# Layer norm of a two-layer trunk: variance summed with tokens on partitions, root and reciprocal once for each token

## What is computed

```python
def layer_norm(x, g, b):
    xc = x - jnp.mean(x, -1, keepdims=True)
    var = jnp.mean(xc * xc, -1, keepdims=True)
    return xc * lax.rsqrt(var + LN_EPS) * g + b

# layer l, m = SiLU(cond) @ w_mod[l] + b_mod[l]
x <- layer_norm(ALPHA * x + 0.5 * gate0 * swiglu(modulate(x, m, 0)))
x <- layer_norm(ALPHA * x + gate1 * mixer(modulate(x, m, 1)))        # conv, then DeltaNet
x <- layer_norm(ALPHA * x + 0.5 * gate2 * swiglu(modulate(x, m, 2)))
# conv mixer: ... a = silu(layer_norm(dwconv(a))) ; a @ w2 + b2
```

## Time and profile before

| | before |
|---|---|
| median of 3 runs | 1921.97 us |
| lowest, highest | 1919.72, 1922.42 us |
| profiled execution, its time | 1926.03 us |
| profiled execution, its span | 1924.3 us |
| PE busy | 1811.4 us, 94% |
| DVE busy | 1028.3 us, 53% |
| ACT busy | 788.7 us, 41% |
| POOL busy | 265.9 us, 14% |
| DMA, mean over the span | 132 GB/s |

### The profile page before, as it was taken

The page is one execution under the profiler, slowest core; times in us unless marked ns, Lnnn a source line. Parts: engine busy times, 40 slices in busy tenths (PEclk is TensorE's granted clock), DMA queues, the critical chain, the costliest instruction groups (busy, mean ns, idle before and its releaser), DMA issues.

```text
span 1924.3 us, 30512 instructions
## 1 busy us (share of the span) xinstructions
PE 1811.4 (94%) x11079; PEld 1664.8 (87%) x11079; DVE 1028.3 (53%) x1780; ACT 788.7 (41%) x1238; POOL 265.9 (14%) x317
## 2 busy tenths in 40 slices
PE   5999999987799999999999999899899999999998
PEld 3899999676578999988999998888788867999997
DVE  4433444899683344455444448766555447443444
ACT  2333332655453444235444326454444335444322
POOL 2000000576320000010000003000222222000001
PEclk8999999998899999999999999999899889999999
DMA  9764444754556443456444445422000024444440
GB/s 323 220 217 129 118 135 142 252 191 126 170 197 207 127 127 114 140 168 195 131 129 117 135 142 146 131 56 66 9 11 11 11 92 130 118 122 131 133 127 35
DMA packets 369962, 254.13 MB, mean 132 GB/s; under 512 B 9716, under 2 KB 350308, under 8 KB 369892
## 3 DMA queue, kind: packets, MB, share of 16 engines
q1 hardware_dynamic: 369104, 252.89, 43.2%
q10 hardware_dynamic: 787, 0.32, 0.1%
HBM read 250.55 MB, written 2.62 MB: 132 GB/s over the span
## 4 chain that ended last, share of the span: by engine, by line
PE 76%; DVE 14%; issue 3%; ACT 2%; DMA 2%; SPq 1%; DVEq 0%; POOL 0%; ACTq 0%
PE bank L1476 22%; PE bank L1478 22%; PE bank L1477 22%; DVE conv L1065 3%; PE bank L1539 2%; DVE tap_odd L1065 2%; DVE w_lo L969 2%; DMA mod_raw<-in_w_mod 1%; SPq L458 1%; PE bank L1747 1%; DVE rstd L1033 1%; PE bank L1503 1%; PE bank L1681 1%; PE bank L1715 1%; PE bank L1724 1%
## 5 line engine op out<-in xcount | busy, mean ns | idle before, releaser
L1476 PE MATMUL bank<-h_hi,w_hi 128*128 128x384 f32 x1920 | 656.2, 342 | 5.6 <-POOL h_lo L587 3.0
L1478 PE MATMUL bank<-h_hi,w_lo 128*128 128x384 f32 x1920 | 645.4, 336 | 0.0
L1477 PE MATMUL bank<-h_lo,w_hi 128*128 128x384 f32 x1920 | 645.0, 336 | 0.0
L969 DVE TENSOR_TENSOR w_lo<-w_raw,w_hi 128x1024 fp32r<-128x1024 f32 x336 | 430.5, 1303 | 191.3 <-ACT w_hi L712 189.6
L712 ACT ACTIVATE w_hi<-w_raw 128x1024 fp32r<-128x1024 f32 x336 | 344.3, 1050 | 314.4 <-PE bank L1478 295.0
L1476 PEld LDWEIGHTS bank<-h_hi,w_hi 128*128 128x128 f32 x1920 | 362.9, 189 | 40.3 <-issue 31.1
L1477 PEld LDWEIGHTS bank<-h_lo,w_hi 128*128 128x128 f32 x1920 | 363.1, 189 | 0.1
L1478 PEld LDWEIGHTS bank<-h_hi,w_lo 128*128 128x128 f32 x1920 | 362.6, 189 | 0.0
L1478 PE MATMUL bank<-act_hi,w_lo 128*128 128x384 f32 x704 | 235.9, 335 | 0.0
L1477 PE MATMUL bank<-act_lo,w_hi 128*128 128x384 f32 x704 | 235.8, 335 | 0.0
L1476 PE MATMUL bank<-act_hi,w_hi 128*128 128x384 f32 x704 | 235.8, 335 | 0.0
(11 more groups left out here) (305 smaller groups left out, 1796.2 us busy)
## 6 DMA issues: line engine op xcount, KB each, us to landing
w_raw<-in_ffn_w_in SPq DMA_DIRECT2D x176, 512.0 KB, 4.7
mod_raw<-in_w_mod SPq DMA_DIRECT2D x132, 512.0 KB, 5.5
w_raw<-in_ffn_w_out SPq DMA_DIRECT2D x64, 448.0 KB, 3.5
w_raw<-in_ffn_w_out SPq DMA_DIRECT2D x32, 512.0 KB, 3.7
w_raw<-in_dn_w_in SPq DMA_DIRECT2D x32, 512.0 KB, 4.0
w_raw<-in_cv_w SPq DMA_DIRECT2D x24, 512.0 KB, 4.1
mod_early<-in_w_mod SPq DMA_DIRECT2D x12, 512.0 KB, 9.7
w_raw<-in_dn_w_out SPq DMA_DIRECT2D x8, 512.0 KB, 4.0
```

The costliest lines, as they stand in the source:

```text
L969: dve.tensor_tensor(w_lo[:, slot], w_raw[:, slot], w_hi[:, slot].bitcast(F32), ALU.subtract).then_inc(w_lo_ready, 1)
L1476: pe.matmul(ps, w_hi[:, w_slot, k], a_hi, start=start, stop=False)
L1477: pe.matmul(ps, w_hi[:, w_slot, k], a_lo, start=False, stop=False)
L1478: return pe.matmul(ps, w_lo[:, w_slot, k], a_hi, start=False, stop=stop)
```

## The change

The variance is summed with the tokens on the partitions. Each of the three blocks of 128 tokens is the stationary operand, a column of `mean_w` the moving one: six products of one column give three columns of variances, one token to a partition, in the free columns T to T+NT of the same bank. ACT and DVE take root and reciprocal of these 128 x 3 values into a new tile `tok_rstd`. PE then spreads them: for each block, `tok_rstd`'s column repeated over 128 columns is the stationary operand and the identity the moving one, which puts the value of token t into column t on all partitions. The result stays in PSUM (`rstd_ps`, columns 0 to T of bank 5), and the multiplies of `normalise` and of the conv module read it there.

A semaphore `tok_ready` tells PE that the reciprocal is there; `rstd_ready` is now given by PE. On PE only slice 4 of the first group stays right behind the variance products; slices 5 to 7 come behind the spread. Where there is no group, 3 warming products take the place of 2 and 10. At the end 6 warming products take the place of 10, and no longer behind a wait.

```diff
+        tok_rstd = sb("tok_rstd", [P, NT])
...
-        mean_ps, var_ps = bank[4], bank[5]
+        mean_ps, var_ps, rstd_ps = bank[4], bank[5], bank[5][:, 0:T]
...
+        tok_ready = sem("tok_ready")
...
                 act.wait_ge(var_added, norm + 1)
-                act.activation(rstd[:, :], var_ps[:, 0:T], ACT.Sqrt, bias=eps[:, :]).then_inc(dev_ready, 1)
+                act.activation(tok_rstd[:, :], var_ps[:, T:T + NT], ACT.Sqrt, bias=eps[:, :]).then_inc(dev_ready, 1)
...
                 dve.wait_ge(dev_ready, norm + 1)
-                dve.reciprocal(rstd[:, :], rstd[:, :]).then_inc(rstd_ready, 1)
+                dve.reciprocal(tok_rstd[:, :], tok_rstd[:, :]).then_inc(tok_ready, 1)
                 dve.wait_ge(rstd_ready, norm + 1)
...
-                    dve.tensor_tensor(conv[:, o], conv[:, o], rstd[:, :], ALU.mult).then_inc(conv_normed, 1)
+                    dve.tensor_tensor(conv[:, o], conv[:, o], rstd_ps, ALU.mult).then_inc(conv_normed, 1)
...
-                    dve.tensor_tensor(r[:, o], r[:, o], rstd[:, :], ALU.mult).then_inc(normed, 1)
+                    dve.tensor_tensor(r[:, o], r[:, o], rstd_ps, ALU.mult).then_inc(normed, 1)
...
-                for j, done in enumerate((sum_g, sum_v)):
+                for done in (sum_g, sum_v):
                     pe.wait_ge(done, 3 * norm + 3)
-                    mm = pe.matmul(var_ps[:, 0:T], mean_w[:, :], squares_at[4 * j], start=(j == 0), stop=(j == 1))
+                for t in range(NT):
+                    for j in range(2):
+                        mm = pe.matmul(var_ps[:, T + t:T + t + 1], squares_at[4 * j][:, t * P:(t + 1) * P], mean_w[:, 0:1], start=(j == 0), stop=(j == 1))
                 mm.then_inc(var_added, 1)
                 for g in beside[:1]:
-                    for k in range(BEFORE_NORM, KC):
+                    mod_slice(g, 0, BEFORE_NORM)
+                if not beside:
+                    keep_warm(3)
+                pe.wait_ge(tok_ready, norm + 1)
+                for t in range(NT):
+                    mm = pe.matmul(rstd_ps[:, t * P:(t + 1) * P], tok_rstd[:, t:t + 1].to_broadcast([P, P]), ident[:, :], start=True, stop=True)
+                mm.then_inc(rstd_ready, 1)
+                for g in beside[:1]:
+                    for k in range(BEFORE_NORM + 1, KC):
                         mod_slice(g, 0, k)
-                if not beside:
-                    keep_warm(2)
-                pe.wait_ge(dev_ready, norm + 1)
-                if not beside:
-                    keep_warm(10)
-                pe.wait_ge(rstd_ready, norm + 1)
-                keep_warm(10)
+                keep_warm(6)
```

## The result

The changed kernel took 1927.97 us (median of 9 runs, 1926.52 to 1933.66) beside 1922.42 of the kernel before on the same chip (9 runs): a ratio of 1.0032, interval 1.002 to 1.0044. It is slower by some 6 us, where 4.4 us less was forecast. Its profiled execution took 1927.97 us, its span 1926.3.

What follows compares the result with a forecast made beforehand. Tensor engine bounds (three quarters of the chain of waits), so norms pay only where it starves: 1.0 + 1.0 one-group norms, 1.4 conv, 1.0 last, 3 x 0 two-group: 4.4 us, median 1921.97 to 1917.6; range 1914.8 to 1921.6.

Steps and rivals of the forecast that it cites:

- The sum of the norm: Norm with a weight split: new products, root, reciprocal and spread bring the first multiply about 1.0 us earlier.
- Products: Six one-column variance products: sums there 1.6 us after the start against 0.95, so 0.65 later; bounds 0.4 to 1.6.
- Reciprocal's end to the multiply: The new spread through the tensor engine: 1.1 us, bounded from 1.0 to 1.6.
- rival 4: Multiplies reading the spread from PSUM are dearer: 31 ns each, 18 in all, 0.56 us, time 1918.1; chance 0.04.
- The one-group norms and the last: Norms after stages 3 and 4, and the last norm: each gains 1.0 us from the earlier first multiply.
- slices, spread and warming still leave no pause over 1 us: Tensor engine around the norms: argument against the clock falling, which would cost 7.5 us.
- rival 5: Tensor clock falls as chunks begin: 1.5 us in each of five norms, 7.5, less the 4.4: 1925; chance 0.07.
- its two reasons: Why the clock might fall: 4 warming products fewer per norm (13 in the last), and one-column products put in.
- the DMA train taken as 0: Second group's slice loads in the three two-group norms: wait grows by the gain; 0 each, within +0.8 and -0.65.
- Rival 2: Late slices stretch the train by load latency: three norms end 0.65 later, at the outermost 1.6; 1919.5; chance 0.18.
- come by bytes, so only the late start of the first, 0.65, can move the end: Second group's four slice loads, 1.7 us apart at 305 GB/s: bytes pace them, so the end moves 0.65 at most.
- the conv norm's 1.4: Conv norm, without a weight split ahead of the reciprocal: first multiply at 506.55, not 507.93, a gain of 1.4 us.

Runs made afterwards that it cites:

- e1: Changed kernel with five warming products filling the pause between the waits for GpSimd's and the vector engine's sums; 1924.55 us, ratio 1.0015 to the kernel before.
- e2: Changed kernel with 10 warming products at the end of the norm in place of 6; 1929.36 us, ratio 1.0035 to the kernel before.
- e8: Changed kernel with the one-column products taken sum by sum, GpSimd's three as soon as that sum is there; 1922.33 us, ratio 1.0.
- e14: Changed kernel with variance products of 128 columns, taken sum by sum; 1921.57 us, ratio 0.9986 to the kernel before.
- e13: Changed kernel with variance products of 128 columns in place of one, pause and order kept; 1927.42 us, ratio 1.0017 to the kernel before.
- e4: Kernel before plus six unread one-column products right behind the wide variance products, no pause added; 1924.76 us, ratio 1.0012.
- e5: Changed kernel with slice 4 (warming products where no group) in the pause, slice 5 behind the one-column products, 6 and 7 behind the spread; 1924.2 us, ratio 1.0001.
- e15: e14 with slice 4 between the two sums, 5 and 6 ahead of the wait for the reciprocal, 7 behind the spread; 1919.69 us, ratio 0.9977.
- e16: Slices placed as in e15 in the three two-group norms, as in e14 in the others; 1916.45 us, ratio 0.9963 to the kernel before.
- e12: Changed kernel with the two weight loads ahead of the second group's slices 0 to 3 on SP's queue; 1928.45 us, ratio 1.0023.
- e3: Kernel before with both 384-column variance products waiting for both sums, which puts the pause in; 1928.53 us, ratio 1.0032.
- e11: e8 plus two warming products ahead of the second sum and weight loads ahead of the second group's slices 0 to 3; 1925.45 us, ratio 1.0.
- e6: e1 with slice 5 as well as slice 4 ahead of the wait for the reciprocal; 1923.1 us, ratio 1.0 to the kernel before.
- e10: e1 with the two weight loads ahead of the second group's slices 0 to 3 on SP's queue; 1924.84 us, ratio 1.0005.

## Why the prediction was wrong

**The sum of the norm was right, step by step.** Products: 1.50 us from the first (339.47) to the root (340.97), 1.6 forecast. Root 0.26, reciprocal 0.17, as forecast. Reciprocal's end to the multiply 1.02 in e1 (342.47 to 343.49), 1.1 forecast (with a slip: 5 x 0.11 + 0.38 is 0.93 and not 0.95, on which nothing hangs). Multiply from PSUM 545 ns: rival 4 is out. (The dearer PSUM access of the Trainium skill, VectorE: DVE Perf Modes, TRN2 errata, is not seen in these rows.) In e1 after stage 0 the first multiply came 1.05 earlier and the first unit 0.75 (forecast 1.0 and about 0.5). The one-group norms and the last gave 3.2 in e1, forecast 3.0. All this holds only with the clock at 1.00.

**First failed step: "slices, spread and warming still leave no pause over 1 us"**, by which rival 5, the falling clock, got 0.07. It looked behind the sums only. The pause is ahead of them: the old first wide product ran between GpSimd's sum and the vector engine's; the diff moves it behind both waits, and I costed the products there but not the 1.4 us that they left empty. The rival's price was 7.5 us, 1.5 in each of five norms; filling the pause (e1) gave back 3.3 us in time, and 6.6 by the norms of the two profiled executions (7.3 less 0.7). Of its two reasons, fewer warming products at the end was wrong (e2); the one-column products were a part of it (e8 against e14), and the pause, which it did not see, another (e13 against e14).

**Second failed step: the DMA train taken as 0, within +0.8 and -0.65 each.** With the clock held behind the sums (e1) the three two-group norms end 2.1, 0.7 and 1.6 later, the first of them with a low stretch among its chunks. Late slices alone cost 1.7 and 1.1 where no low stretch came in (e4, after stages 0 and 1). Rival 2 was right in sign, and its outermost 1.6 was near; its reason, the latency of a load, no run tried. It was weighed as an alternative to rival 5, and both came. I argued that the loads "come by bytes, so only the late start of the first, 0.65, can move the end". The runs speak against that: e5 has the first earlier, the third 0.7 to 1.3 later and no gain, while with the first three ahead of their old times or within 0.2 us of them (e15) the loss went from 2.9 to 0.2, though 2.2 of this belong to the norm with the low stretch. So later buffers count as well as the first, and while they came free late after stage 2 the DMA engines moved less (193 to 281 GB/s in e1, 264 to 387 before); how the loss divides among the four stays open.

**Third, smaller: the conv norm's 1.4.** With the pause filled it gave 0.5: the clock was low ahead of its sums as before, and the warming products ran at that clock and held the sums up; without any there (e8, e14) it gave 1.1 to 1.2.

From forecast to result are 10 us. The clock is 3.3 of them (e1 against the changed kernel), the train 4.4 (with what the low stretch after stage 0 cost), the conv norm 0.9; the first is from times, the others from norms. The rest, over 1 us, is less than the two kinds lie apart, and I can't place it. What stays open: why the clock, with the same order, falls in some norms and not in others (e8, e13), and what clock stretches among the chunks (e14 and e16, after stage 1) owe to the waits for loads just ahead of them; neither was tried by itself.

## What to carry to other kernels

When a diff moves an instruction behind a later wait, look at what its engine now does in the place that it left, not only at what the instruction costs in the new one. Work that merely releases a buffer can have its own due time: list each release with the load that waits for it before moving any. And a faster chain is worth its sum only if the engine that it feeds stays at its clock: read the granted clock of each stretch, and compare kernels norm by norm.

## What the runs showed of the hardware

An fp32 product with one column was no cheaper here than one with 128, where each product has its own weights of 128 x 128: 0.11 us a half with one column (ten halves from 339.47 to 340.57) and with 128 (e13). That the weight load sets this is my reading. So the wider form cost nothing, and in the same order it lowered the clock in none of six outer norms where the narrow one lowered it in three (e14 and e8).

The tensor clock falls more easily than I thought. Behind a pause of 1.1 to 1.4 us followed by one-column products it fell in six outer norms of six (the changed kernel), and in e2 and e12 in five and, from ahead of the sums on, in the last. With the pause and wider products it fell in three and, from ahead of the sums on, in the last (e13, 128 columns) or in one (e3, 384 columns). With one-column products and no pause over 0.6 us it fell in three (e8), in four and, from ahead, in the last (e11), or in none (e4, where the variance itself is summed by the wide products). With neither it fell behind the sums in none (e14, e15, e16), and in none where five warming products filled the pause ahead of narrow ones (e1, e6, e10); with one slice there it held in three norms and fell in two (e5). A single profile of each stands behind these counts, and they do not say which norm will fall. But every execution has its granted clock over the whole span on record, and the means agree: 0.976 to 0.977 in the kernel before and in e4, e15 and e16, 0.975 in e3, e6 and e14, 0.974 in e1, e10 and e13, 0.971 in e8 and e11, and 0.967 to 0.969 in the three kernels with pause and one-column products. All nine executions of the changed kernel lie at 0.971 or below, all of e14 at 0.972 or above.
